# FFN entry by token halves, weight tiles between modulation chunks, and modulation sums a few tiles later, in a one-layer decoder kernel on one Trainium2 core

## The chip, the cores and the metric

The kernel runs on one core of one Trainium2 chip. The time is the device time of one execution in microseconds. Before the change it is 1890.21 us, the median of three runs (1888.95, 1891.62 and 1890.21). TensorE multiplies, ScalarE (ACT) and VectorE (DVE) work on tiles in SBUF and PSUM, GpSimd (POOL) does small work here, and SyncE (SP) issues all loads. PE stands for TensorE in the profile.

## The reference

One decoder layer over 256 tokens of width 2048, in float32:

```
mod = silu(c) @ w_ada + b_ada                     # 6 x 2048: shift, scale, gate for mixer and FFN
h = rmsnorm(x) * g * (1 + sc_m) + sh_m
y = token_mixer(h)                                # HGRN2 recurrence and latent attention from one projection,
                                                  # each with an output projection, sigmoid-gated sum, @ w_out
x = x + ga_m * rmsnorm(y)
h = rmsnorm(x) * g * (1 + sc_f) + sh_f
y = (silu(h @ w_gate) * (h @ w_up)) @ w_down      # inner width 5632
x = x + ga_f * rmsnorm(y)
```

## The kernel before

**Products.** Activations are kept transposed, channels on the partitions: `hT_hi` and `hT_lo` hold 16 blocks of 128 channels by 256 tokens. Each float32 product is made of three matmuls in a shorter format: high by high, high by low, low by high. So each weight tile (`raw`, 128 x 1024, two blocks of 128 channels by 512 columns, 512 KB) is loaded by SyncE, turned into `whi` by ScalarE (function `high`, line 465) and into `wlo` by VectorE (function `low`, line 1225), and multiplied by TensorE for both token halves (function `multiply`, lines 839 to 841): 2 halves x 2 blocks x 3 = 12 matmuls of 512 columns. A group of tiles (8 for 2048 channels) accumulates in a pair of PSUM banks, one bank for each half of 128 tokens; two pairs take turns.

**The ring.** There are four slots of `raw`, `whi` and `wlo` (`RING`). SyncE requests tile c when `low` of tile c - 4 is done (semaphore `lo_ready`); `high` of tile c waits for its landing and until tile c - 4 has been multiplied (`multiplied`). ScalarE and VectorE run three tiles ahead (`AHEAD`).

**Order.** Nothing is scheduled at run time: each engine's program is a written list of steps numbered by tile, with side work tied to a tile number. All engines work in order, so whatever stands behind a waiting instruction of its engine waits too. SyncE is one such queue.

**First phase** (up to about 250 us). Four quarters of 20 tiles. Each needs the shift and scale of its channels: 16 modulation chunks of 512 KB (`ada0`, function `load_ada0`) are multiplied by `silu(c)` and accumulated by VectorE (line 1232), and summed over the partitions by 16 matmuls of one column (`sum_rows`, line 874). There are ten chunk slots. SyncE requests 16 chunks, weight tiles 0 to 3, ten more chunks, the key weights and the masks (lines 367, 368), and then one tile at a time with as many chunks as `ada_due` lets VectorE consume. The sum of the second quarter follows tile 13.

**Output projections.** 32 tiles each, for attention (`place_om`, about 834 to 942) and recurrence (`place_oh`, up to 1035). Beside them, 16 chunk pieces each of later modulation columns are accumulated: VectorE takes piece r after `low` of tile `ADA_OM[r]` or `ADA_OH[r]`; SyncE requests it four tiles after piece r - 2 was taken. There are two chunk slots. TensorE sums after tile 23, VectorE reads the sums (`piece`) at step 26 or 27. At tile 8 of the second projection SyncE requests x once more (2 MB, into `att`, called `x2`).

**FFN entry.** The last projection (`place_out`, 32 tiles of `w_out`) ends at 1122.9 us. Then ScalarE squares the last outputs (line 704), VectorE applies a gain (1650), sums, and with POOL takes the reciprocal root (`rsqrt_of`, 1284 and 792), mixes in the residual (`x2`, 1682), ScalarE squares x2 (`square_sum`, 476), a second root gives two diagonal matrices (`by_rms`, 1688), and TensorE multiplies x2 with them (function `transpose_x2`, 1143): this transposes and normalises, 8 pairs of channel blocks with 8 instructions each. ScalarE applies scale and shift (735) and makes the high part (739), VectorE the low part (1694). The first gate tile is multiplied when the first pair is ready; pairs 4 to 7 are transposed after gate tiles 0 to 3.

Of the kernel before, what the change touches and what calls it, by code (L numbers as in the profile page):

```python
# [30 lines left out]
P = 128  # L31
# [26 lines left out]
ADA_SLOTS = 10  # L58
ADA_PACE = [(0, 0), (15, 16), (20, 21), (35, 32), (55, 48), (80, 48)]
# [55 lines left out]
def build(nc, x, vectors, consts, masks, positions, ada0, ada1, ada2, ga_bias, post_rows, w_start, w_kr, w_uqn, w_uqr, w_uk, w_uv, w_hf,  # L115
          w_hq, w_hi, w_hg, w_omla, w_ohg, w_out, w_gate, w_up, w_down, out):
    ctx = ExitStack()
    with ctx:
# [181 lines left out]
        ADA_OH = [4, 5, 6, 7, 8, 9, 10, 12, 13, 14, 15, 17, 18, 20, 21, 22]  # L300
# [32 lines left out]

        block = ctx.enter_context(nc.Block())
# [3 lines left out]
        def _(sp):  # L338
# [119 lines left out]
        def _(act):  # L458
# [249 lines left out]
            for c in range(GD * CD + AHEAD):  # L708
# [7 lines left out]
                if i == 3 and j == 1:  # L716
                    copy_gain(0)

            for tt in range(TT):
                act.wait_ge(sig("x_mixed"), tt + 1)  # L720
                if tt:
                    act.wait_ge(sig("x2_squared"), tt)
                square_sum(x2[:, tt], all_dec, stat[:, 10 + tt:11 + tt]).then_inc(sig("x2_squared"), 1)
            first = Place(B_FF, G_FF)
            for kp in range(KD // 2):
                if kp == 0 or kp > AHEAD:
                    high(first, max(kp, AHEAD))
                act.wait_ge(sig("scale_h_ready"), PH + 1)
                act.wait_ge(sig("x2_transposed"), kp + 1)
                if kp >= 2:  # L730

                    act.wait_ge(sig("h2_low"), kp - 1)
                for j in range(2):
                    k = 2 * kp + j
                    nc.scalar.activation(dec[:, kp % 2, j * T:(j + 1) * T], PS[:, XA + kp % 4, j * T:(j + 1) * T],
                                         ACT.Identity, scale=scale_h[:, k:k + 1], bias=mods[:, SH_F + k:SH_F + k + 1])\
                      .then_inc(sig("h2_scaled"), 1)
                act.wait_ge(sig("h2_scaled"), 2 * kp + 2)
                nc.scalar.activation(pairs(hT_hi, kp), dec[:, kp % 2, 0:NW], ACT.Copy)\
                  .then_inc(sig("h2_high"), 1)  # L740
# [47 lines left out]
        def _(pool):  # L788
# [22 lines left out]
            power(stat[:, 8:8 + TT], TT, "trunk", 1)  # L811

# [1101 lines left out]
```

## Time and profile before

| | |
|---|---|
| median of three runs | 1890.21 us |
| profiled execution, its own time | 1886.96 us |
| its span | 1885.1 us |
| TensorE busy | 1822.5 us (97%) |
| VectorE busy | 1296.2 us (69%) |
| ScalarE busy | 891.3 us (47%) |
| GpSimd busy | 104.3 us (6%) |
| loaded from HBM | 420.36 MB, 224 GB/s over the span |

The span runs from the first to the last instruction of one profiled execution; all positions in the text are microseconds from its start. A busy TensorE is not TensorE at full speed: its matmuls take twice as long where the granted clock is 0.50. What bounds the kernel is read from where TensorE waits, for whom, and where its clock is low.

### The profile page before, as it was taken

To read this page: it belongs to the slowest core of one execution; us is meant where nothing else is said; L and a number is where in the kernel's file an instruction comes from. 1 tells how busy PE (TensorE), PEld (TensorE's weight loads), DVE (VectorE), ACT (ScalarE), POOL (GpSimd) and SP (SyncE) were. 2 spreads that over 40 slices of the span, in tenths; PEclk is the share of its full clock that TensorE was granted. 3 is DMA by queue.
4 is the path that set the end of the run, shared out by engine and by line. 5 is a ranking of instruction groups with operands and counts; after the bars stand their busy time and mean duration, and the time that the engine had idled before them with its cause. 6 is when DMAs were issued, how large, how long until landed. Compare 5 with 4: busy or idle time off the path is not lost.

```text
span 1885.1 us, 24326 instructions
## 1 busy us (share of the span) xinstructions
PE 1822.5 (97%) x8828; PEld 1529.7 (81%) x8828; DVE 1296.2 (69%) x1361; ACT 891.3 (47%) x1007; POOL 104.3 (6%) x72
## 2 busy tenths in 40 slices
PE   3999999999999999999999989999999999999997
PEld 2788888888888888888778867888888888888886
DVE  7799768678668668669677554666656666665557
ACT  5544555645645645644334446444443444443443
POOL 0000000120120120220000000000000000000000
PEclk9999999999999999999999999999999999999999
DMA  9997548646646647547786654666666666665553
GB/s 383 409 366 254 191 156 291 237 162 227 233 156 231 226 156 244 180 167 268 242 317 226 219 179 138 223 222 230 212 227 230 212 222 219 228 212 176 193 190 131
DMA packets 115985, 423.38 MB, mean 225 GB/s; under 512 B 13008, under 2 KB 13392, under 8 KB 115408
## 3 DMA queue, kind: packets, MB, share of 16 engines
q1 hardware_dynamic: 115920, 422.51, 65.3%
q8 instruction: 42, 0.69, 0.2%
q14 instruction: 23, 0.19, 0.0%
HBM read 420.36 MB, written 2.10 MB: 224 GB/s over the span
## 4 chain that ended last, share of the span: by engine, by line
PE 89%; DVE 5%; DMA 4%; issue 1%; ACT 1%; SPq 0%; POOL 0%; DVEq 0%; ACTq 0%; POOLq 0%
PE PS L839 27%; PE PS L841 26%; PE PS L840 26%; DMA ada_raw<-in_ada 2%; PE PS L986 2%; DVE ada_acc L1232 2%; DMA raw<-in_w_start 2%; PE PS L848 1%; DVE wlo L1225 1%; PE PS L874 1%; PE PS L1032 1%; PE PS L1031 1%; PE PS L1143 0%; PE PS L857 0%; PE PS L866 0%
## 5 line engine op out<-in xcount | busy, mean ns | idle before, releaser
L1225 DVE TENSOR_TENSOR wlo<-raw,whi 128x1024 fp32r<-128x1024 f32 x600 | 732.5, 1223 | 415.7 <-ACT whi L465 414.2
L465 ACT ACTIVATE whi<-raw 128x1024 fp32r<-128x1024 f32 x600 | 630.1, 1053 | 743.2 <-PE PS L841 658.3
L839 PE MATMUL PS<-whi,hT_hi 128*128 128x512 f32 x1792 | 707.6, 395 | 8.6 <-DVE wlo L1225 5.4
L841 PE MATMUL PS<-whi,hT_lo 128*128 128x512 f32 x1792 | 699.1, 390 | 0.0
L840 PE MATMUL PS<-wlo,hT_hi 128*128 128x512 f32 x1792 | 698.7, 390 | 0.0
L839 PEld LDWEIGHTS PS<-whi,hT_hi 128*128 128x128 f32 x1792 | 337.3, 188 | 77.9 <-issue 6.0
L841 PEld LDWEIGHTS PS<-whi,hT_lo 128*128 128x128 f32 x1792 | 336.9, 188 | 71.1
L840 PEld LDWEIGHTS PS<-wlo,hT_hi 128*128 128x128 f32 x1792 | 337.4, 188 | 67.4 <-issue 0.2
L839 PE MATMUL PS<-whi,cT_hi 128*128 128x512 f32 (+1 forms) x592 | 231.5, 391 | 2.0 <-DVE side L1549 1.5
L840 PE MATMUL PS<-wlo,cT_hi 128*128 128x512 f32 (+1 forms) x592 | 227.9, 385 | 0.0
L841 PE MATMUL PS<-whi,cT_lo 128*128 128x512 f32 (+1 forms) x592 | 227.9, 385 | 0.0
L1232 DVE SCALAR_TENSOR_TENSOR ada_acc<-ada_raw,csilu,ada_acc 128x512 f32<-128x512 f32 (+1 forms) x185 | 141.3, 764 | 32.5 <-DMA ada_raw<-in_ada 28.8
L839 PEld LDWEIGHTS PS<-whi,cT_hi 128*128 128x128 f32 x592 | 111.7, 189 | 25.9 <-issue 3.5
L841 PEld LDWEIGHTS PS<-whi,cT_lo 128*128 128x128 f32 x592 | 111.7, 189 | 22.3
L840 PEld LDWEIGHTS PS<-wlo,cT_hi 128*128 128x128 f32 x592 | 111.7, 189 | 21.9 <-issue 0.7
L1397 DVE TENSOR_TENSOR gate<-gate,PS 128x1024 f32<-128x1024 f32 x64 | 78.1, 1220 | 14.5 <-PE PS L841 14.2
L792 POOL TENSOR_TENSOR stat<-stat,con 128x2 f32<-128x2 f32 (+2 forms) x11 | 13.8, 1258 | 1329.4 <-DVE stat L1284 1211.7
L199 POOL TENSOR_TENSOR dec<-bT 128x512 f32<-128x512 f32 x24 | 47.1, 1964 | 392.8 <-DVE bT L1490 333.4
L1530 DVE COPY_PREDICATED pT<-msk,PS 128x512 f32<-128x512 uint8 x28 | 25.1, 896 | 33.6 <-issue 27.2
L986 PEld LDWEIGHTS PS<-zT 128*128 128x128 f32 x384 | 46.2, 192 | 1.6
L986 PE MATMUL PS<-zT 128*128 128x64 f32 x384 | 45.4, 271 | 0.0
L1752 DVE SCALAR_TENSOR_TENSOR gate<-ada_raw,csilu,gate 128x1024 f32<-128x1024 f32 x32 | 40.9, 1279 | 0.0
(228 smaller groups left out, 1052.0 us busy)
## 6 DMA issues: line engine op xcount, KB each, us to landing
ada_raw<-in_ada SPq DMA_DIRECT2D x142, 512.0 KB, 4.8
raw<-in_w_gate SPq DMA_DIRECT2D x88, 512.0 KB, 4.1
raw<-in_w_up SPq DMA_DIRECT2D x88, 512.0 KB, 4.2
raw<-in_w_down SPq DMA_DIRECT2D x88, 512.0 KB, 4.1
raw<-in_w_start SPq DMA_DIRECT2D x80, 512.0 KB, 4.9
raw<-in_w_hf SPq DMA_DIRECT2D x32, 512.0 KB, 3.9
raw<-in_w_hq SPq DMA_DIRECT2D x32, 512.0 KB, 5.0
raw<-in_w_hi SPq DMA_DIRECT2D x32, 512.0 KB, 4.5
```

Source lines behind the costliest of these rows:

```text
L199: eng.tensor_tensor(d[:, :, 1, :], b[:, :, 1, :], end, ALU.subtract)
L465: nc.scalar.activation(whi[:, pl.slot(c), 0:w], raw[:, pl.slot(c), 0:w], ACT.Copy)\
L839: nc.tensor.matmul(o, hi[:, kt, tok], whi[:, s, cols], start=start, stop=False)
L840: nc.tensor.matmul(o, hi[:, kt, tok], wlo[:, s, cols], start=False, stop=False)
L841: last = nc.tensor.matmul(o, lo[:, kt, tok], whi[:, s, cols], start=False, stop=stop)
L848: last = nc.tensor.transpose(PS[:, bank + h // 2, ((h % 2) * TT + tt) * P:][:, 0:P], src[:, tt, h * P:(h + 1) * P], ident)
L986: last = nc.tensor.matmul(PS[:, XA + L % 4, i * 64:(i + 1) * 64], z[:, i], zt[:, i, :, 1, :], start=True, stop=True)
L1225: nc.vector.tensor_tensor(wlo[:, s, 0:w], raw[:, s, 0:w], whi[:, s, 0:w].bitcast(F32), ALU.subtract)\
L1232: last = nc.vector.scalar_tensor_tensor(out=acc, in0=slot, scalar=csilu[:, a:a + 1], in1=acc, op0=ALU.mult, op1=ALU.add)
L1397: nc.vector.tensor_tensor(dst, dst, banks(2 * p), ALU.add).then_inc(pair_free[p], 1)
L1530: nc.vector.copy_predicated(o, mask.unsqueeze(1).broadcast_to(shape), PS[:, XA + L % 4, :].rearrange("p (i x m) -> p i x m", i=2 * HPG, m=m))\
L1752: nc.vector.scalar_tensor_tensor(out=acc, in0=ada_raw[:, q % 2], scalar=csilu[:, bass.ds(n * 2 + (q // 2 - 2), 1)], in1=acc, op0=ALU.mult, ...
```

## The change

There are three parts.

First phase: SyncE requests three chunks (`ADA_FIRST`) behind weight tiles 0 to 3 and not ten; from then on, the lead of the chunk requests grows by one with every third tile, up to ten. Key weights and masks are requested after tile 24.

Output projections: in the first, the sum follows tile 25 and not 23, goes to PSUM bank `XA + 3`, and is read at step 27. In the second, the chunk pieces are taken at other tiles, the sum follows tile 26, and is read at step 28. The waits of the row transposes that use these banks move with them.

FFN entry: the last four tiles of `w_out` are multiplied for the first 128 tokens (`tt` = 0), all four, and then for the other 128. Squares, gain, root, mixing, squares of x2, root and diagonal are done for each half by itself. The first four channel pairs are transposed, scaled and split for each half by itself (list `H2`: 8 half units, then 4 whole ones), and gate tiles 0 to 3 are multiplied first for half 0, then for half 1. ScalarE's and VectorE's orders are written out anew.

```diff
+ADA_FIRST = 3
-        ADA_OH = [4, 5, 6, 7, 8, 9, 10, 12, 13, 14, 15, 17, 18, 20, 21, 22]
+        ADA_OH = [6, 7, 8, 9, 10, 13, 14, 15, 17, 18, 21, 22, 23, 24, 25, 26]
+        H2 = [(kp, slice(tt * P, (tt + 1) * P)) for tt in range(TT) for kp in range(4)] + [(kp, slice(0, T)) for kp in range(4, KP)]
...
-            for a in range(KD, KD + ADA_SLOTS):
+            asked = KD + ADA_FIRST
+            for a in range(KD, asked):
                 load_ada0(a)
-            sp.dma_start(key_weights, w_kr).then_inc(sig("kr_loaded"), 16)
-            sp.dma_start(msk[:], masks).then_inc(sig("masks_loaded"), 16)
...
-                    for a in range(KD + ada_due(c - RING) + ADA_SLOTS, KD + ada_due(c - RING + 1) + ADA_SLOTS):
-                        if a < ADA0:
-                            load_ada0(a)
+                    ahead = KD + ada_due(c - RING + 1) + min(ADA_SLOTS, ADA_FIRST + (c - RING) // 3)
+                    for a in range(asked, min(ahead, ADA0)):
+                        load_ada0(a)
+                    asked = max(asked, min(ahead, ADA0))
+                    if c == SG * W_G + RING:
+                        sp.dma_start(key_weights, w_kr).then_inc(sig("kr_loaded"), 16)
+                        sp.dma_start(msk[:], masks).then_inc(sig("masks_loaded"), 16)
```

ScalarE after tile 31 of `w_out` (`square_out_rows` squares one half of the last outputs, `square_x2` one half row of x2, `h2_high` scales and converts one unit):

```diff
+            square_out_rows(0)
+            high(first, 0)
+            high(first, 1)
+            square_x2(0, 0)
+            square_x2(0, 1)
+            square_out_rows(1)
+            high(first, 2)
+            h2_high(0)
+            h2_high(1)
+            square_x2(1, 0)
+            h2_high(2)
+            square_x2(1, 1)
+            h2_high(3)
+            high(first, 3)
+            for u in range(4, 8):
+                h2_high(u)
+            for u in range(8, len(H2)):
+                high(first, u - 4)
+                h2_high(u)
```

TensorE (`multiply_rows` is `multiply` for one half):

```diff
-                if c == 23:
+                if c == 25:
                     pe.wait_ge(ada_step, ADA0 + 2 * S_OM + 2 * ADA_N)
                     for r, acc in enumerate(ada_sum):
-                        last = sum_rows(acc, XA, r * HPG)
+                        last = sum_rows(acc, XA + 3, r * HPG)
...
-            for c in range(N_ST):
+            for c in range(N_ST - RING):
...
+            for tt in range(TT):
+                for kp in range(CD - RING, CD):
+                    hi, lo, home = row_home(2 * KP + kp)
+                    last = multiply_rows(pl, GD - 1, CD, (GD - 1) * CD, kp, tt, hi, lo, kt0=KC * (home - kp))
+                    if tt:
+                        last.then_inc(multiplied, 1)
+                if tt == 0:
+                    last.then_inc(sig("out_rows"), 1)
...
+            for u in range(4):
+                transpose_x2(u)
+            for c in range(4):
+                if c == 3:
+                    for u in range(4, 8):
+                        transpose_x2(u)
                 pe.wait_ge(sig("h2_low"), c + 1)
+                multiply_rows(first, 0, CD, 0, c, 0, hT_hi, hT_lo)
+            for c in range(4):
+                pe.wait_ge(sig("h2_low"), 4 + c + 1)
+                multiply_rows(first, 0, CD, 0, c, 1, hT_hi, hT_lo).then_inc(multiplied, 1)
+                transpose_x2(8 + c)
+            for c in range(4, CD):
+                pe.wait_ge(sig("h2_low"), 4 + c + 1)
                 multiply(first, 0, CD, 0, c, c + 1, hT_hi, hT_lo)
```

VectorE (`y_rms` and `x2_rms` are the roots of one half, the gain multiply of the half stands inside `y_rms`; `mix_x2` mixes half a row of one half):

```diff
+            y_rms(0)
...
+            mix_x2(0, 0)
+            mix_x2(0, 1)
+            low(first, 0)
+            x2_rms(0)
+            y_rms(1)
+            dve.wait_ge(pair_free[1], freed_by(1, G_FF))
+            mix_x2(1, 0)
+            low(first, 1)
+            h2_low(0)
+            mix_x2(1, 1)
+            h2_low(1)
+            low(first, 2)
+            h2_low(2)
+            x2_rms(1)
+            h2_low(3)
+            low(first, 3)
             dve.wait_ge(sig("scale_h_ready"), PH + 1)
+            for u in range(4, 8):
+                h2_low(u)
+            for u in range(8, len(H2)):
+                low(first, u - 4)
+                h2_low(u)
```

## Rows read from the trace of the kernel before

**Rows 1.** The page, part 1: busy us, share of span, count of instructions.
```profile
PE 1822.5 (97%) x8828; PEld 1529.7 (81%) x8828; DVE 1296.2 (69%) x1361; ACT 891.3 (47%) x1007; POOL 104.3 (6%) x72
```

**Rows 2.** Busy time by stretch: stretch, its length, busy us by engine, clock, DMA.
```profile
105.00:850.00 745.00, 743.51 (x3949) 635.74 (x3948) 554.93 (x649) 399.64 (x485) 93.06 (x61) 1.00 0.63 214
...
1157.00:1870.00 713.00, 713.00 (x3184) 590.15 (x3184) 441.69 (x369) 294.27 (x286) 3.53 (x1) 1.00 0.63 210
```

**Rows 3.** Waits of TensorE: total us, times, longest us.
```profile
PE PS L839 <- DVE wlo L1225: 5.9, 4, 3.0
PE PS L874 <- DVE ada_acc L1232: 4.2, 2, 2.8
```

**Rows 4.** Timeline of TensorE where it waits: start, us, instruction, [wait before <- releaser].
```profile
54.70 0.47 PE L839 MATMUL PS<-whi,hT_hi 128*128 128x512 f32 x1 [3.00 <-DVE wlo L1225]
...
82.80 1.95 PE L874 MATMUL PS<-con,mixed 128*128 128x1 f32 x16 [0.64 <-DVE mixed L1232]
...
907.72 1.95 PE L874 MATMUL PS<-con,ada_acc 128*128 128x1 f32 x16 [1.46 <-DVE ada_acc L1232]
...
958.67 0.47 PE L839 MATMUL PS<-whi,hT_hi 128*128 128x512 f32 x1 [1.78 <-DVE wlo L1225]
...
968.05 0.50 PE L839 MATMUL PS<-whi,hT_hi 128*128 128x512 f32 x1 [0.65 <-DVE wlo L1225]
```

**Rows 5.** Busy time by stretch around low clocks (third last column: PEclk).
```profile
54.70:58.10 3.40, 3.40 (x15) 2.83 (x16) 3.25 (x3) 1.81 (x2) 0.00 (x0) 1.00 1.03 411
82.80:86.20 3.40, 3.40 (x23) 3.15 (x24) 3.40 (x4) 2.52 (x3) 0.00 (x0) 1.00 1.03 411
909.70:913.10 3.40, 3.40 (x9) 2.63 (x9) 2.57 (x4) 0.00 (x0) 0.00 (x0) 0.50 0.92 287
...
1134.90:1138.40 3.50, 3.45 (x16) 3.48 (x17) 1.23 (x2) 1.28 (x3) 0.00 (x0) 0.50 0.31 112
1138.40:1141.80 3.40, 3.40 (x25) 3.14 (x25) 1.38 (x2) 3.34 (x7) 0.00 (x0) 1.00 0.10 39
```

**Rows 6.** Timelines of ScalarE and VectorE, first phase.
```profile
52.24 1.06 ACT L465 ACTIVATE whi<-raw 128x1024 fp32r<-128x1024 f32 x1 [10.91 <-DMA raw<-in_w_start]
...
80.07 2.67 DVE L1232 SCALAR_TENSOR_TENSOR mixed<-ada_raw,csilu,mixed 128x1024 f32<-128x1024 f32 x2
```

**Rows 7.** Second projection: request and landing of x; timeline of VectorE.
```profile
att<-in_x SPq DMA_DIRECT2D x1, 2048.0 KB, 10.4
...
907.58 2.35 DVE L1225 TENSOR_TENSOR wlo<-raw,whi 128x1024 fp32r<-128x1024 f32 x2
...
955.84 1.54 DVE L1232 SCALAR_TENSOR_TENSOR ada_acc<-ada_raw,csilu,ada_acc 128x512 f32<-128x512 f32 x2 [5.81 <-DMA ada_raw<-in_ada]
957.30 1.22 DVE L1225 TENSOR_TENSOR wlo<-raw,whi 128x1024 fp32r<-128x1024 f32 x1
```

**Rows 8.** Timelines of ScalarE, VectorE and TensorE at the FFN entry.
```profile
1120.28 1.06 ACT L465 ACTIVATE whi<-raw 128x1024 fp32r<-128x1024 f32 x1 [1.66 <-PE PS L841]
1122.94 0.60 ACT L704 ACTIVATE dec<-PS 128x512 f32<-128x512 f32 x1 [1.60 <-PE PS L841]
...
1126.79 4.62 DVE L1682 SCALAR_TENSOR_TENSOR att<-gate,stat,att 128x2048 f32<-128x2048 f32 x2 [0.81 <-POOL stat L792]
...
1131.43 1.91 ACT L476 ACTIVATE dec<-att 128x2048 f32<-128x2048 f32 x1 [0.26 <-DVE att L1682]
...
1134.95 5.45 PE L1143 MATMUL PS<-stage,att 128*128 128x128 f32 x32 [12.04 <-DVE stage L1688]
...
1137.09 1.02 ACT L735 ACTIVATE dec<-PS,mods,scale_h 128x256 f32<-128x256 f32 x2 [2.71 <-PE PS L1143]
...
1138.71 1.02 ACT L735 ACTIVATE dec<-PS,mods,scale_h 128x256 f32<-128x256 f32 x2
...
1151.05 0.48 PE L839 MATMUL PS<-whi,hT_hi 128*128 128x512 f32 x1
...
1154.68 0.47 PE L839 MATMUL PS<-whi,hT_hi 128*128 128x512 f32 x1
```

More of the change, by code:

```diff
@@ L706, in square_out @@
                       .then_inc(sig("y_squared"), 1)
-            for c in range(GD * CD + AHEAD):
+            for c in range(GD * CD):
                 high(pl, c)
@@ L717, in _, with square_out_rows @@
                     copy_gain(0)
-            for tt in range(TT):
-                act.wait_ge(sig("x_mixed"), tt + 1)
+            first = Place(B_FF, G_FF)
+            junk = side[:].rearrange("p t c -> p (t c)")
+            def square_out_rows(tt):
                 if tt:
[L722 to L727, printed above, removed]
+                    act.wait_ge(multiplied, pl.through(N_ST - 1))
+                    act.wait_ge(sig("x2_squared"), 2)
+                else:
+                    act.wait_ge(sig("out_rows"), 1)
+                act.wait_ge(sig("y_squared"), (GD - 1) * TT + tt)
+                nc.scalar.activation(junk[:, 0:NW], PS[:, 2 * pl.pair(GD - 1) + tt, :], ACT.Square,
+                                     accum_out=sums[:, tt, GD - 1:GD]).then_inc(sig("y_squared"), 1)
@@ L1124, in _, with multiply_rows @@
             pl = place_out
-            for c in range(N_ST):
+            def multiply_rows(pl, g, n, c0, c, tt, hi, lo, kt0=0):
+                p = pl.pair(g)
+                if c == 0 and tt == 0:
+                    pe.wait_ge(pair_free[p], pl.freed(g))
+                pe.wait_ge(lo_ready, pl.through(c0 + c))
+                s = pl.slot(c0 + c)
+                for k in range(KC):
+                    kt = kt0 + c * KC + k
+                    tok = slice(tt * P, (tt + 1) * P)
+                    cols = slice(k * NW, (k + 1) * NW)
+                    o = PS[:, 2 * p + tt, :]
+                    start, stop = c == 0 and k == 0, c == n - 1 and k == KC - 1
+                    nc.tensor.matmul(o, hi[:, kt, tok], whi[:, s, cols], start=start, stop=False)
+                    nc.tensor.matmul(o, hi[:, kt, tok], wlo[:, s, cols], start=False, stop=False)
+                    last = nc.tensor.matmul(o, lo[:, kt, tok], whi[:, s, cols], start=False, stop=stop)
+                return last
+            for c in range(N_ST - RING):
                 if c == CD:
@@ L1653, in gain_pair @@
                   .then_inc(pair_free[p], 1)
-            for c in range(AHEAD, GD * CD + AHEAD):
+            for c in range(AHEAD, GD * CD):
                 low(pl, c)
@@ L1680, in _, with gain_rows_out @@
-            dve.wait_ge(pair_free[1], freed_by(1, G_FF))
-            for tt in range(TT):
-                nc.vector.scalar_tensor_tensor(out=x2[:, tt], in0=ya[:, tt], scalar=stat[:, 8 + tt:9 + tt],
-                                               in1=x2[:, tt], op0=ALU.mult, op1=ALU.add)\
-                  .then_inc(sig("x_mixed"), 1)
-            dve.wait_ge(sig("x2_squared"), TT)
-            rsqrt_of(stat[:, 10:10 + TT], D, "trunk", 2)
-            for tt in range(TT):
+            def gain_rows_out(tt):
+                if tt:
+                    dve.wait_ge(multiplied, pl.through(N_ST - 1))
+                else:
+                    dve.wait_ge(sig("out_rows"), 1)
+                cols = slice((GD - 1) * NW, GD * NW)
+                p = pl.pair(GD - 1)
+                nc.vector.tensor_tensor(ya[:, tt, cols], PS[:, 2 * p + tt, :], post_gain[0][:, cols], ALU.mult)\
+                  .then_inc(pair_free[p] if tt else sig("y_scaled"), 1)
@@ L1689, in _ @@
                   .then_inc(sig("rms_diagonal"), 1)
[L1690 to L1701 removed]
+            first = Place(B_FF, G_FF)
```

108 lines of the change are left out of this document (62 added, 46 removed).

## The prediction

> **What bounds the kernel now.** Read the engine shares first: TensorE is busy for 1822.5 of 1885.1 us [rows 1], so whatever the change gives has to come out of the remaining 62.6 us or out of stretches at half clock. The busy time by stage then shows where not to look: from 105 to 850 us TensorE misses 1.5 us of 745, from 1157 to 1870 nothing of 713 [rows 2]. The table of waits then names, beside the start: 5.9 us in four waits for a low weight half, 4.2 us in two waits for modulation sums [rows 3]. The timeline of TensorE places those that the diff can reach: 3.00 us at 54.70, 0.64 at 82.80, 1.46 at 907.72, 1.78 at 958.67 and 0.65 at 968.05 [rows 4]; the fourth wait for a low half is what is left of the 5.9, 0.5 us, and 12.04 us stand at 1134.95, before the transposes of the FFN entry [rows 8]. (The 2.8 us that are left of the 4.2 lie before the first weight tile is multiplied and are not edited.) Last, the granted clock by stretch: 1.00 after the wait of 3.00 us, but 0.50 from 909.7 to 913.1 and in the first 3.5 us after work restarted at 1134.9, then 1.00 [rows 5].
>
> So a tile's 12 matmuls set the pace: on ScalarE 1.06 us of work and 1.66 us of waiting for TensorE make 2.72 us a tile [rows 8]. ScalarE's conversion and VectorE's subtraction (1.22 us, [rows 7]) hide in that, and only the places above pay.
>
> **First phase.** Before, ten modulation chunks, the key weights and the masks stand in SyncE's queue between weight tile 3 and tile 4. At 411 GB/s [rows 5] a 512 KB piece takes 1.28 us, so that is 11.1 pieces or 14.3 us; ScalarE waits 10.91 us for tile 4's landing at 52.2 [rows 6], and TensorE 3.00 us. After, three chunks stand there: tile 4 lands 8.1 pieces or 10.4 us earlier, near 42, and is no longer late. The sum behind the 0.64 us waits for VectorE's last two chunks of the second quarter, 80.07 to 82.74 [rows 6]; these follow the subtraction of tile 14. Ahead of that tile stand 15 weight and 20 chunk pieces plus 1.1 of key weights and masks now, 15 and 16 after: 5.1 pieces, 6.5 us sooner, less what the DMA engines idle because tiles 5 to 7 wait for free ring slots (three handovers of about 1 us: I take 2.5). Net 4 us sooner against the 3.0 us by which TensorE comes sooner, so this wait goes too: 3.64 us. No matmul, conversion or byte is removed. What is late next is tile 26: there the lead of the chunks is back at ten, the key weights have been requested, and the DMA backlog is as before while TensorE is 3.6 us ahead. Before, tile 26 was needed near 117.2 (84.6 after the sum, 12 tiles of 2.72); its piece is the 44th behind tile 4's, landing near 52.2 + 56.3 = 108.5 before and after; with 2.5 us of idle 111.0, with conversion and subtraction 113.4, against a need at 113.6. Nothing to spare, so the bound is 1.6 us lost again. I take 3.6, ends 2.0 and 3.7.
>
> **Modulation sums of the output projections.** The first sum moves from tile 23 to tile 25 and to another bank. Its last chunk ends on VectorE just before 907.72 [rows 4]; TensorE would now reach the sum at 906.3 + 2 x 2.72 + 0.6 of transposes = 912.3, so the 1.46 us go. The subtractions of tiles 25 and 26 end at 908.7 and 909.9 [rows 7], each before its turn (909.0, then after the sum). The half clock behind the sum goes with the wait, I think: the stretch of 3.4 us at half clock [rows 5] does 1.7 us of work. After the wait of 0.64 us with the same 16 one-column matmuls at 82.80 the clock stayed at 1.00 [rows 5], and the new sum has no wait at all. Gain 3.2, ends 1.4 (clock still falls) and 3.2. The added wait is VectorE's read of the sum at step 27, for which it now stands some 3 us; behind it are a gating multiply and the subtraction of tile 28, which end about 2.7 us after TensorE starts tile 26, two tiles before tile 28 is due. SyncE's next request waits for that subtraction and lands within its 11 us of ring.
>
> In the second projection the chunks move two tiles later at the start, so that chunk pieces 2 and 3 are requested with tiles 10 and 11 and not 8 and 9, behind the 2 MB of x, which take 10.4 us to land [rows 7]. Before, VectorE stood 5.81 us for such a piece at 955.84 [rows 7], with tile 8's subtraction queued behind it. After, tile 8's subtraction comes at about 951, before any chunk that x delays; x ends near 949.5, tiles 9 and 10 at 950.7 and 952.0, the next piece at 953.3, each further one at 1.28 us, or 4 after its request. Worked on, subtractions 9 to 12 end at 956.0, 958.7, 962.7 (a gated pair of 1.2 us each follows) and 966.2; TensorE needs them at 959.4, 962.1, 964.9 and 967.6. Slack 3.4, 3.4, 2.2, 1.4: all three waits, 1.78 + 0.65 + 0.5 = 2.9 us, go. Six chunks in a row (21 to 26) let VectorE fall behind by some 0.5 us a tile, 3 of its 5.7 us of lead, and the sum now waits until after tile 26. I take 2.9, ends 1.0 and 2.9.
>
> **FFN entry.** Call the end of the last output tile T (1122.9). Before: squares, gain, reciprocal root, mixing (4.62 us for two rows of 2048), squares of x2 (1.91 each), a second root and two diagonals follow one another, 12.04 us to the first transpose; 32 transpose instructions take 5.45 us mostly at half clock, and the fifth gate tile starts at 1154.68 [rows 8], T + 31.8.
>
> After, the last four output tiles run token half 0 first, so its outputs are whole at T - 5.44. By the durations of [rows 8]: square 0.60 and the reading of its sum, 0.75 (T - 4.65); reduce, scale and root 1.3 (T - 3.3), the half's gain multiply (0.65 by the 1.22 for 1024) beneath it; two mixings of 1024 at 1.28 [rows 6] (T - 0.8); ScalarE's squares of them 1.25 each, the last at T + 0.75; reduce, scale, POOL, diagonal 1.6: T + 2.35. The first transposes start there: 9.7 us less waiting. Then VectorE's queue sets the pace: y's root for half 1, its gain multiply, a mixing (T + 4.7), subtraction of gate tile 1 (T + 5.85), and only then the first low part of h2: tile 0, half 0, at T + 6.3. A mixing and a low part put tile 1 at T + 7.9, a subtraction and a low part tile 2 at T + 9.45. ScalarE (1.62 us from one whole unit to the next; a half has 512 elements less in its three instructions, at 0.85 ns by the squares of 512 and 2048: 1.18 us) ends half 1's squares at T + 9.0; root and diagonal T + 10.9; 16 transposes 1.8 (T + 12.75); tile 3's half 1.36, T + 14.1. From there TensorE has all its operands: four halves 5.44 and four transpose units at 3.63 - 2.72 = 0.9, 3.6 in all, so the fifth gate tile starts at T + 23.1. That is 8.7 us sooner at full clock. Work is the same: 64 transposes, 96 matmuls; about 5.5 us of waits remain.
>
> What the clock adds: waits of about 2.35 and 2.1 us stand around 1.8 us of transposes. Rows speak both ways: full clock after 3.00 us of waiting, half after 1.46 us and a sum [rows 4, 5]. One stretch of 3.4 us at half clock costs 1.7 us less the small waits that it fills. I take 1.2, nearest to one stretch; the lower end is two stretches, 3.4. If half-size instructions cost ScalarE as much as whole ones, four units lose 1.8 us more. Entry: 7.5, ends 8.7 - 3.4 - 1.8 = 3.5 and 8.7.
>
> **Sum.** 3.6 + 3.2 + 2.9 + 7.5 = 17.2 us. The profiled execution took 1886.96 us for its span of 1885.1, so it would be 1869.8. The median of the runs is 1890.21, 3.25 above: 1873.0.
>
> **The rivals.**
> A, chance 15%: the entry gains only about 3.5. For it: VectorE carries both halves' chains and the weight subtractions in one queue, and TensorE works in pieces of 1.4 us at an uncertain clock. Against: half 0's chain ends before T. 1873.0 + 4.0 = 1877.0.
> B, 13%: waits move rather than go in the early parts: tile 26 is late by 1.6, the sum is followed by the low clock (1.7), the second projection keeps 1.9. 1873.0 + 5.2 = 1878.2.
> C, 4%: every short piece of the entry runs at half clock: two times four half units of transposes, 1.8 each, and three halves of tiles, 4.1, once more, of which 0.8 fills waits, 6.9 lost, so the entry gains 1.8: 1873.0 + 5.7 = 1878.7. For it: the half clock behind a wait and a sum at 909.7; against it: 1.00 behind 3.00 us of waiting [rows 5]. The Trainium skill (TensorE: Matmul & The Clock Gate, section HAM oscillation) describes this: matmul groups shorter than the waits between them start at the low clock each time. The row at 909.7 agrees, that at 54.7 does not.
> D, 2%: the change does not do what it says: the low part of half 0 comes after half 1's mixing, and the entry is no shorter. With B's losses, 1873.0 + 7.5 + 5.2 = 1885.7.
> E, 3%, slower: stop and go keeps the clock at half from the first transposes to the end of the gate group. That is 1.8 + 1.8 + 5.4 + 5.4 + 3.6 + 10.9 = 28.9 us of work, once more 28.9, less 4 us that fill waits, against the 1.2 in my sum: 1873.0 + 23.7 = 1896.7. It decides from some 18 us more than forecast, so about 22 us of such work at half. Against it: the clock was back 3.5 us after the restart at 1134.9 [rows 5].
> The forecast keeps 63%, with its own range of 1869.5 to 1876.5.
>
> **From these to the numbers.** Cases are told apart from no change at about 0.2%, 3.8 us. Forecast, A, B and C are faster, 0.95, of which I give 0.01 to what none of them names; within 0.2%, or just at its line, is D and that: 0.03; slower is E: 0.03. The range reaches up past A, B and C, and down by 3.5: the terms at their good ends give 1.3, and single runs of one kernel differ by up to 2.7 (1888.95 to 1891.62). So 1869.5 to 1880.5.
>
> **What will show it.** No wait above 0.3 us on TensorE between 50 and 100 us; none before the sum near 912, and a clock of 1.00 behind it; none between 950 and 970. At the entry, first transposes 2.3 us after the last output matmul, three or four waits summing to 5.5 us, at most one stretch at 0.50, and the fifth gate tile 23 to 25 us after T. Wrong would be: a wait near tile 26 of the first phase, VectorE still in the mixing of half 1 when T + 6.3 has passed, or a clock of 0.50 beyond T + 12.

## The result, and the profile after

The changed kernel takes 1869.12 us, median of four runs (1867.67 to 1872.3), against 1889.58 us for the kernel before (four runs, 1888.45 to 1891.62): ratio 0.9893, 95% interval 0.9876 to 0.991. It is faster, by 20.5 us. The forecast was 1873.0 with a range of 1869.5 to 1880.5, so the time lies 0.4 us below the range: the direction was right and the gain was put too low. Its own single runs spread over 4.6 us, more than that distance.

The profiled execution after took 1872.3 us, the slowest of its four, and that of before, 1886.96, lay under all its other first runs. The two profiles are therefore only 14.7 us apart. The experiments below give each kernel a second profile, and the reading rests on both pairs.

The page after, part 1:
```profile
PE 1823.1 (97%) x8828; PEld 1531.2 (82%) x8828; DVE 1296.6 (69%) x1373; ACT 893.8 (48%) x1023; POOL 105.0 (6%) x74
```
TensorE has the same 8828 matmuls as in [rows 1] and works as long; the span is shorter because it waits less. Its waits between 30 and 1200 us, after (total us, times, longest):
```profile
PE PS L891 <- issue: 3.0, 1, 3.0
PE PS L926 <- DVE ada_acc L1319: 2.2, 1, 2.2
PE PS L1222 <- DVE stage L1786: 2.2, 1, 2.2
PE PS L891 <- DVE side L1636: 1.5, 3, 0.5
PE PS L891 <- DVE stage L1484: 1.2, 1, 1.2
PE PS L1191 <- DVE hT_lo L1794: 1.0, 1, 1.0
PE PS L891 <- DVE side L1484: 0.8, 1, 0.8
PE PS L891 <- DVE wlo L1312: 0.3, 1, 0.3
```
Of [rows 3], the 5.9 us for low weight halves are down to 0.3, and of the 4.2 us for modulation sums the 2.2 at the start are left. The wait of 12.04 us at the entry [rows 8] has become 2.2 and 1.0. Two rows are new, both for L1484: VectorE's addition of a finished pair of banks to `stage` or `side`, which frees the pair.

The timeline of TensorE after, at the places of [rows 4, 8]:
```profile
40.37 0.77 PE L891 MATMUL PS<-whi,hT_hi 128*128 128x512 f32 x1 [3.01 <-issue]
...
80.26 1.84 PE L926 MATMUL PS<-con,mixed 128*128 128x1 f32 x16
...
110.63 0.50 PE L891 MATMUL PS<-whi,hT_hi 128*128 128x512 f32 x1 [1.16 <-DVE stage L1484]
...
117.21 0.50 PE L891 MATMUL PS<-whi,hT_hi 128*128 128x512 f32 x1 [0.81 <-DVE side L1484]
...
139.13 1.06 PE L926 MATMUL PS<-con,ada_acc 128*128 128x1 f32 x9
...
909.53 0.50 PE L891 MATMUL PS<-whi,cT_hi 128*128 128x512 f32 x1 [0.29 <-DVE wlo L1312]
...
917.36 0.60 PE L909 MATMUL PS<-con,mixed 128*128 128x128 f32 x4
...
990.46 0.71 PE L909 MATMUL PS<-con,gate 128*128 128x128 f32 x5
...
1117.94 2.64 PE L1222 MATMUL PS<-stage,att 128*128 128x128 f32 x16 [2.21 <-DVE stage L1786]
1121.56 0.80 PE L1191 MATMUL PS<-whi,hT_hi 128*128 128x512 f32 x1 [0.98 <-DVE hT_lo L1794]
...
1140.02 0.48 PE L891 MATMUL PS<-whi,hT_hi 128*128 128x512 f32 x1
```
No wait stands at tile 4, at the sum of 80.26, or in the second projection. The first transposes of the FFN entry start 2.21 us behind the last output product, the fifth gate tile (1140.02) 24.3 us behind it, where it was 31.8.

Busy time by stretch after (stretch, length, busy us by engine, clock, DMA share, GB/s); it answers to [rows 5]:
```profile
909.70:913.10 3.40, 3.40 (x20) 2.85 (x20) 2.04 (x2) 0.95 (x2) 0.00 (x0) 1.00 0.66 186
1119.17:1126.00 6.83, 5.85 (x19) 4.63 (x18) 6.14 (x11) 6.70 (x17) 0.54 (x1) 0.50 0.31 109
1126.00:1129.40 3.40, 3.40 (x23) 3.05 (x22) 1.26 (x2) 1.25 (x4) 0.00 (x0) 1.00 0.37 136
```
At 909.7 TensorE does 20 matmuls in 3.4 us at full clock where it did 9 at half; at the entry 6.83 us are at half clock.

### The profile page after: what moved, and what is told of

Read it like the earlier page. It is cut to its first block and busy times, and to the rows that moved or that the text cites. A ratio compares the mean times of both kernels' runs of the same rounds, so it can differ in the third digit from the quotient of the medians.

```text
span 1870.4 us, 24368 instructions
## 1 busy us (share of the span) xinstructions
PE 1823.1 (97%) x8828; PEld 1531.2 (82%) x8828; DVE 1296.6 (69%) x1373; ACT 893.8 (48%) x1023; POOL 105.0 (6%) x74
## 5 line engine op out<-in xcount | busy, mean ns | idle before, releaser
L891 PE MATMUL PS<-whi,hT_hi 128*128 128x512 f32 x1760 | 694.3, 395 | 5.0 <-issue 3.0
L893 PE MATMUL PS<-whi,hT_lo 128*128 128x512 f32 x1760 | 686.2, 390 | 0.0
L892 PE MATMUL PS<-wlo,hT_hi 128*128 128x512 f32 x1760 | 685.8, 390 | 0.0
L891 PEld LDWEIGHTS PS<-whi,hT_hi 128*128 128x128 f32 x1760 | 331.0, 188 | 72.6 <-issue 3.3
L893 PEld LDWEIGHTS PS<-whi,hT_lo 128*128 128x128 f32 x1760 | 330.8, 188 | 69.8
L892 PEld LDWEIGHTS PS<-wlo,hT_hi 128*128 128x128 f32 x1760 | 331.2, 188 | 66.4 <-issue 0.2
L845 POOL TENSOR_TENSOR stat<-stat,con 128x1 f32<-128x1 f32 (+2 forms) x13 | 14.6, 1123 | 1318.3 <-DVE stat L1371 1200.5
L1484 DVE TENSOR_TENSOR gate<-gate,PS 128x1024 f32<-128x1024 f32 x64 | 78.0, 1218 | 14.6 <-PE PS L893 14.3
```

The costliest lines, as they stand in the source:

```text
L891: nc.tensor.matmul(o, hi[:, kt, tok], whi[:, s, cols], start=start, stop=False)
L892: nc.tensor.matmul(o, hi[:, kt, tok], wlo[:, s, cols], start=False, stop=False)
L893: last = nc.tensor.matmul(o, lo[:, kt, tok], whi[:, s, cols], start=False, stop=stop)
L1484: nc.vector.tensor_tensor(dst, dst, banks(2 * p), ALU.add).then_inc(pair_free[p], 1)
```

## The experiments

The kernel before had a median of 1888.86 us in the first group of runs (15 runs), 1887.97 in the second (9) and 1888.85 in the third (27). Each ratio is against it.

**The changed kernel once more.** No edit.

> The changed kernel once more. Theory (the sum by parts is right on the traces, and single executions differ by where the clock's half-speed stretches fall at the start of the span): median again about 20 us under before, single times spread over 3 to 5 us, and the profiled one need not lie at the median. In its trace the waits of the FFN entry and of tiles 24 to 26 of the first phase return within 0.2 us, while the first weight tile starts anywhere from 38.5 to 40.5 us. Rival (one of the two profiled executions was not typical in a part after the start): the fifth gate tile or the output projections come at another distance, by over 1 us, from what stands before them.

1869.1 us (1868.13 to 1870.61), ratio 0.99 (0.9885 to 0.9915). The times and the waits at tiles 24 and 26 (1.1 and 0.9 us) came back as the theory said. At the entry the rival is right: the second wait is 0.4 us and not 1.0, and the fifth gate tile starts 22.6 us behind the last output product, where it was 24.3.

**The kernel before once more.** No edit.

> The kernel before, once more, for a second profile. Theory 1 (its first profile was a cheap execution): the times lie at 1888.9 like the other runs of before; this profile shows the same waits of the matrix engine as the first (2.66 at 54.70, 2.1 at 82.80, 1.48 at 907.7, some 2.9 in four behind the second projection) and other stretches at half clock, 20 to 31 us of them ahead of the last where the first had 20.5. Rival (the profile costs time or saves it in every execution): its waits are the same too, but so are the half stretches, and the time again lies 2 to 3 us under the median of the unprofiled runs.

1889.53 us (1885.77 to 1891.14, ten runs), ratio 1.0003 (0.9994 to 1.0012); its profiled execution took 1887.94. The times lie where the other runs of before do, and the clock differs, so theory 1 holds for the clock. It does not for the waits: the one before tile 4 is 0.83 us where the first profile had 3.00, since this execution starts its first weight tile at 40.40 and that one at 38.60. TensorE in this second profile of before, timeline and then stretches:
```profile
40.40 0.76 PE L839 MATMUL PS<-whi,hT_hi 128*128 128x512 f32 x1 [3.01 <-issue]
54.11 0.47 PE L839 MATMUL PS<-whi,hT_hi 128*128 128x512 f32 x1 [0.83 <-DVE wlo L1225]
...
909.37 2.10 PE L874 MATMUL PS<-con,ada_acc 128*128 128x1 f32 x16 [1.53 <-DVE ada_acc L1232]
...
958.18 0.39 PE L841 MATMUL PS<-whi,cT_lo 128*128 128x512 f32 x1
960.11 0.47 PE L839 MATMUL PS<-whi,hT_hi 128*128 128x512 f32 x1 [1.54 <-DVE wlo L1225]
960.42 0.40 PE L840 MATMUL PS<-wlo,hT_hi 128*128 128x512 f32 x1
960.66 0.39 PE L841 MATMUL PS<-whi,hT_lo 128*128 128x512 f32 x1
960.89 0.40 PE L839 MATMUL PS<-whi,hT_hi 128*128 128x512 f32 x1
...
1135.77 5.69 PE L1143 MATMUL PS<-stage,att 128*128 128x128 f32 x32 [12.04 <-DVE stage L1688]
```
```profile
85.00:88.41 3.41, 3.41 (x10) 2.67 (x9) 3.38 (x6) 2.25 (x4) 0.00 (x0) 0.50 1.02 406
...
911.02:914.43 3.41, 3.41 (x10) 2.76 (x10) 2.92 (x4) 0.00 (x0) 0.00 (x0) 0.50 0.75 222
...
1126.06:1139.71 13.65, 3.94 (x18) 3.97 (x19) 7.19 (x10) 6.69 (x9) 1.39 (x2) 0.50 0.14 47
```
Behind the sum at 82.8 the clock falls here, from 85.00 to 88.41 (ten matmuls in 3.41 us); in the profile the forecast was made from it stayed at 1.00 over 82.8 to 86.2 with 23 [rows 5]. Six profiles have the old first phase (two of before, and those of the kernels below that leave it alone). All reach this sum at 82.7 to 82.8, however early they start. In four the clock falls at 84.6 to 85.2, and the third sum follows 57.9 us behind this one; in the other two it follows 56.3 us behind. So this stretch costs 1.6 us when it comes, and the forecast was made from an execution without it. Before the last stretch this execution has 30.7 us at half clock (10.24 at the start, 3.41, 3.41, 13.65), the first profile of before had 20.5 (6.83, 3.41, 10.24), the two of after 17.1 and 10.2. The mean granted clock lay between 0.989 and 0.993 in all runs of before, between 0.994 and 0.997 in all of after.

The gain by stage, each the difference of the starts of the same instruction in two traces (third modulation sum, 139.13 above; transposes four tiles behind the first projection, 917.36; transposes in the third projection, 990.46; fifth gate tile, 1140.02):

| stage | forecast | first profiles | second profiles |
|---|---|---|---|
| first phase | 3.6 | 0.0 | 2.0 |
| first projection sum | 3.2 | 2.6 | 3.2 |
| second projection | 2.9 | 4.6 | 3.8 |
| FFN entry | 7.5 | 7.5 | 9.5 |
| all | 17.2 | 14.7 | 18.5 |

The two pairs differ by 2.0 us in the first phase because of the 1.6 us at half clock behind the sum and 0.3 us by which the two executions of the changed kernel differ. Other profiles show how far one pair can be trusted. The third sum comes at 139.1 to 140.8 us with the old first phase (six profiles) and at 138.2 to 140.8 with three early chunks (five). The stretch with the second projection is 3.8 to 5.2 us shorter in each profile with the new list. The fifth gate tile follows 31.8 to 32.6 us behind the last output product with the old entry (six) and 22.6 to 24.3 with the new one (four profiles without further edits there).

**The three parts alone**, each put into the kernel before.

```diff
-            for a in range(KD, KD + ADA_SLOTS):
+            asked = KD + ADA_FIRST
+            for a in range(KD, asked):
```

> The kernel before with the first part alone: three chunks behind tiles 0 to 3, key weights and masks after tile 24. Theory of the first trace (waits near tiles 24 and 26 take back what tile 4's wait gave): 1.9 us faster, with waits of about 1.2 and 0.8 us there. Rival (the forecast, 3.6 us): no wait between 50 and 135 us, and 3.6 us faster.

1887.79 us (1883.01 to 1888.05, eleven runs), ratio 0.9992 (0.9983 to 1.0001): 1.1 us, not told apart from nothing; 3.6 us lie outside the interval, 1.9 inside. In its trace the wait at tile 4 is gone, and waits of 1.15 us at 109.45 and 1.02 us at 116.25 stand in its place, as in the whole change.

```diff
-        ADA_OH = [4, 5, 6, 7, 8, 9, 10, 12, 13, 14, 15, 17, 18, 20, 21, 22]
+        ADA_OH = [6, 7, 8, 9, 10, 13, 14, 15, 17, 18, 21, 22, 23, 24, 25, 26]
...
-                if c == 23:
+                if c == 25:   # first sum; the second one: c == 26
```

> The kernel before with the second part alone: sums after tiles 25 and 26, chunk pieces of the second projection at the later tiles. Theory of the first trace (each wait costs some 0.3 us beyond what it shows, since the pipeline empties and fills): 2.6 us from the first projection, 4.6 from the second, 7.2 in all. Rival (the forecast by the waits alone): 6.1 us. Third: the second projection's gain came from the rest of the change and not from its own tile numbers: under 4 us.

1879.97 us (1879.24 to 1880.84), ratio 0.9957 (0.9943 to 0.9971): 8.9 us where 6.1 were forecast for the two terms; the interval is 5.5 to 10.8 us, so the times alone do not rule out 6.1. In its trace the transposes in the third projection come 7.2 us sooner than in the second profile of before. No wait is left between 850 and 1000 us.

```diff
-            for kp in range(4):
-                transpose_x2(kp)
-            for c in range(CD):
+            for u in range(4):
+                transpose_x2(u)
+            for c in range(4):    # token half 0, then half 1, then whole tiles
```

> The kernel before with the third part alone: FFN entry by token halves. Theory: 7.5 us faster, the fifth gate tile 24.3 us after the last output matmul, two stretches at half clock. Rival (unprofiled executions keep the clock up at the entry, which would explain a median gain above the sum by traces): 9 to 11 us faster.

1880.28 us (1879.6 to 1880.44), ratio 0.9958 (0.9944 to 0.9971): 8.6 us; 7.5 were forecast, and the interval of 5.5 to 10.6 us holds both theories. The trace was expected to show two half stretches and the fifth gate tile at 24.3 us; it shows one (3.41 us) and 23.05. The three alone add up to 18.5, all together give 19.8 (1888.86 less 1869.1): within the intervals the parts are independent.

**The sums one at a time.** The first sum alone (`c == 23` to `25`, other bank, its reading at 27):

> The kernel before with the later modulation sum of the first output projection alone (sum behind tile 25 into another bank, piece at 27). Theory 1 (each wait that goes is worth what the trace shows plus 0.3 us, and the half clock that it brings): the wait of 1.48 and the half stretch at 909.7 go, a gain of 3.3 us at the first sum of the second projection, none behind it: 1885.6. Rival (this sum has no part of its own, half clock comes there anyway): 1.5 us, 1887.4.

1884.98 us (1883.25 to 1887.29, eleven runs), ratio 0.9976 (0.9967 to 0.9985): 3.9 us. Then the second list and sum alone:

> The kernel before with the spread list and the later sum of the second output projection alone (sum behind tile 26, piece at 28). Theory 1 (the four waits go, 2.9 us as shown and 0.3 us each on top, and nothing is late in their place): 4.3 to 4.6 us, 1884.5, and with the other sum alone 7.9 to 8.9 together. Rival (the gain of 4.6 behind tile 12 in the kernel with both comes in part from the first sum, which frees VectorE earlier): 2.9 us, 1886.0, and one wait of over 0.5 us stays in the second projection.

1884.66 us (1882.88 to 1886.93, eleven runs), ratio 0.998 (0.9971 to 0.9989): 4.2 us. Waits of TensorE from 850 to 1000 us, first of the one, then of the other kernel:
```profile
PE PS L839 <- DVE wlo L1225: 4.2, 4, 1.7
```
```profile
PE PS L874 <- DVE ada_acc L1232: 1.2, 1, 1.2
```
With the first sum alone the sum's own wait is gone, and the waits of the second projection are longer than the 2.8 us they were: TensorE comes sooner to the same late chunks. With the second list alone none of them is left. For the second list theory 1 holds (4.3 to 4.6 expected): its trace is 4.2 us ahead of the second profile of before at the third projection, and no wait is left, which speaks against the rival of 2.9, though the interval (2.1 to 5.5 us) does not. For the first sum the time speaks for theory 1 (3.3 expected, 1.5 outside the interval of 2.8 to 6.2), but the claim that nothing follows is wrong by 1.4 us of waits: its trace, of an execution 2.3 us above its median, gains 2.5 us up to the transposes behind the first projection and is only 1.1 ahead at the third. How the median comes to 3.9 is open.

**More chunks early.** The new waits of the first phase should come of idle DMA engines between 42 and 57 us.

```diff
-ADA_FIRST = 3
+ADA_FIRST = 6
```

> The changed kernel with six chunks and not three behind weight tiles 0 to 3 (ADA_FIRST = 6). Theory: the waits near tiles 24 and 26 stem from 4.5 us in which the DMA engines had nothing asked of them between 42 and 57 us, since each request waited for a ring slot; three more chunks (3.8 us) fill that, tile 4 lands near 45 and is still not late, and both waits go: 2.3 us faster than the changed kernel, some 1867. Rival: VectorE's queue makes them (a chunk and the addition of a group stand ahead of each subtraction): they stay, 1869. Rival: a wait before tile 4 returns, and nothing is gained.

1867.75 us (1866.99 to 1870.94), ratio 0.9897 (0.9882 to 0.9913), at most 1.4 us under the changed kernel by medians and within its interval. The DMA engines from 40 to 60 us in slices of half a microsecond (GB/s, and the total), first after, then with six chunks:
```profile
GB/s 393 377 123 33 8 131 295 377 393 418 377 98 131 188 336 369 451 410 410 377 377 303 287 377 377 361 344 377 418 385 426 393 426 418 410 434 426 410 418 401
DMA packets 1844, 6.73 MB, mean 337 GB/s; under 512 B 204, under 2 KB 204, under 8 KB 1843
```
```profile
GB/s 410 426 410 401 402 418 401 418 401 426 410 401 401 410 410 418 401 426 410 410 377 410 401 434 401 410 393 426 401 401 418 418 402 418 393 426 401 402 418 426
DMA packets 2243, 8.19 MB, mean 410 GB/s; under 512 B 246, under 2 KB 246, under 8 KB 2242
```
Three chunks leave two holes, near 41 to 43 and 45.5 to 47 us: 337 of 410 GB/s over 20 us, that is 3.6 us of transfers not made. Six fill them. Then one wait is left between 45 and 135 us, and the third sum starts 3.0 and 2.7 us sooner than in the two profiles of the change. The theory of idle DMA engines holds for the waits; of the 2.3 us that it promised, the medians show 1.4 at most, and the ratios, each against its own group of runs, 0.5:
```profile
79.80 1.95 PE L926 MATMUL PS<-con,mixed 128*128 128x1 f32 x16 [0.60 <-DVE mixed L1319]
...
136.12 1.06 PE L926 MATMUL PS<-con,ada_acc 128*128 128x1 f32 x9
```

**A busy TensorE in the entry's first wait.**

```diff
+            pe.wait_ge(lo_ready, first.through(0))
+            for i in range(9):
+                nc.tensor.matmul(PS[:, XA + 3, :], hT_hi[:, i % 4, 0:P], whi[:, first.slot(0), 0:NW], ...)
```

> The changed kernel with nine matmuls of 512 columns, whose result nobody reads, in TensorE's first wait at the FFN entry (2.0 us of the 2.2). Theory: the half clock at the entry comes of TensorE's doing nothing; with work there it stays at 1.00, and the fifth gate tile comes 22.0 to 22.6 us after the last output matmul in each execution, against 24.3 and 22.6 in the two traces so far: 1 us faster in the median. Rival: the later wait and the short pieces are enough to drop it: no change. Rival: the first transposes come later by the added work and the time rises by up to 0.5 us.

1869.65 us (1868.31 to 1872.25), ratio 0.9901 (0.9886 to 0.9916). TensorE at the entry, timeline and stretches:
```profile
1117.55 2.32 PE L1229 MATMUL PS<-whi,hT_hi 128*128 128x512 f32 x9 [0.23 <-DVE wlo L1315]
1119.70 1.95 PE L1222 MATMUL PS<-stage,att 128*128 128x128 f32 x16
1123.16 0.50 PE L1191 MATMUL PS<-whi,hT_hi 128*128 128x512 f32 x1 [1.51 <-DVE hT_lo L1797]
...
1139.96 0.48 PE L891 MATMUL PS<-whi,hT_hi 128*128 128x512 f32 x1
```
```profile
1116.00:1119.50 3.50, 3.27 (x15) 2.39 (x14) 2.07 (x7) 3.31 (x7) 0.55 (x1) 1.00 0.27 64
1119.50:1123.00 3.50, 2.15 (x18) 1.91 (x16) 3.40 (x5) 2.81 (x8) 0.54 (x1) 1.00 0.22 88
```
The clock stays at 1.00 here, and the fifth gate tile starts 22.6 us behind the last output product (1139.96 less 1117.3). The second profile of the change, with one stretch of 3.41 us at half clock, has 22.6 too; two more profiles with one stretch have 23.1 (six chunks, and the entry alone); the first, with 6.83 us, has 24.3. So one stretch costs 0 to 0.5 us, since full clock mostly turns into waiting for VectorE, and two cost 1.7. The gain of 1 us that was expected of the median did not come. Both edits together:

> The kernel after with six early modulation chunks in place of three and nine idle matrix products of 512 columns in the first wait at the FFN entry. Theory 1 (both edits keep what they gave: 1.3 us in the first phase; at the entry the fifth gate tile 22.6 us behind the last product of the output, against 22.6 with one half stretch and 24.3 with two): 1867.3, 0.5 under first6. Rival (the idle products only take power or issue time: no gain on an average execution): 1868.3. If the gain of first6 was chance of the executions: 1869.1.

1868.15 us (1867.32 to 1868.95), ratio 0.9893 (0.9878 to 0.9908): nothing over six chunks alone, though the granted clock was 1.00 without a break from 44.38 to 1860.27. The rival holds.

**A busy TensorE at the start.** 10 and 14 idle transposes in the two waits before the first weight tile.

```diff
+            keep_busy(10)
             sum_quarter(0)
             pe.wait_ge(sig("xT_copied"), KD // 2)
+            keep_busy(14)
```

> The changed kernel with 24 transposes whose result nobody reads before the first modulation sum (10) and before the first weight tile (14), where TensorE waits 2.2 to 3.1 and 3.0 us. Theory: the clock then stays up from there on; the first 12 to 16 matmuls, now at half, and the sum take 3 us less between them: 2 to 3 us faster, and the single times lie within 2 us of each other, as the alignment of a half-speed stretch no longer matters. Rival: the transposes run at half clock themselves and push the sum and the first tile back: no change, or 1 us slower.

1876.47 us (1874.18 to 1877.26), ratio 0.9937 (0.9923 to 0.995): 7 us slower than the change. The stretch from 36.11 to 42.93 is at 0.50 all the same, though the 14 transposes run from 35.38 on. Up to the third sum (137.83) this profile is still 1.0 and 1.3 us ahead of the two of the change. Then two waits are new, in the loop over the groups:
```profile
495.18 0.79 PE L891 MATMUL PS<-whi,hT_hi 128*128 128x512 f32 x1 [2.11 <-issue]
...
639.28 0.49 PE L891 MATMUL PS<-whi,hT_hi 128*128 128x512 f32 x1 [1.84 <-issue]
```
Stretches of 6.8 and 3.4 us at half clock stand there, and the two places cost 4.6 and 3.6 us against either profile of the change. The waits name no releaser ("issue"), but the trace shows one. In both, TensorE is at the branch that closes the loop (`pe.Fori`, line 1118): it takes 4.02 us at 490.90 and 3.75 us at 635.26, where the same branch takes 0.24 and 0.22 in the changed kernel. And the DMA queue that loads instructions, from 480 to 770 us, reads
```profile
q8 instruction: 18, 0.29, 0.4%
```
while none of the other 13 profiles has a single row of it there: they load seven blocks of 16 KB between 330 and 480 us, in the first turn of the loop, and none in the next two. So the loop's code, which had stayed in place, is loaded again in every turn. The loop itself was not edited; that the instructions ahead of it shifted its code across a block is the likely reason, and was not tried.

**One subtraction earlier.** The subtraction of gate tile 1 goes between the scaling and the root of half 0.

```diff
-            x2_rms(0)
+            x2_rms(0, lambda: low(first, 1))
...
-            low(first, 1)
```

> The changed kernel with the subtraction of gate tile 1 moved, on VectorE, from behind the first mixing of half 1 into its wait for POOL's root of half 0. Theory (VectorE's queue sets the pace of the entry): the first transposes come 0.5 us later, everything from the first low part on 0.6 us earlier, and the second wait of TensorE shrinks by 1 us: 0.6 us faster. Rival (the clock or ScalarE sets the pace from there on): no change. Third: TensorE's first wait grows by 0.5 us and brings a further stretch at half clock: 1 us slower.

1870.29 us (1869.13 to 1872.8), ratio 0.9905 (0.989 to 0.992): no gain. The first transposes wait 3.13 us and not 2.2, the second wait is gone, and the fifth gate tile comes 23.4 us behind the last output product (1140.60 less 1117.15), between the two profiles of the change. The first low part of h2 starts 5.2 us behind that product instead of 5.4, so the 0.6 us that VectorE was to save there is 0.2.

## Why the prediction came out as it did

**The last step failed: 3.25 us added to a sum made from one execution.** The gains were read from an execution of before of 1886.96 us and then set against a median of 1890.21; the 3.25 us between the two were added back as if the change left them alone. The runs show two things in them. First, 1.35 us: the median of three runs stood that far above the 1888.86 of 15 later ones. Second, the remaining 1.9 us: the profiled execution had less half clock than most. Its mean granted clock was 0.993. Of 61 later runs of before only two have that (median 1887.33), 28 have 0.990 (median 1889.75) and 3 have 0.989 (1891.76). The places are known from the profiles: the stretch behind the sum at 82.8, 1.6 us, in four of six profiles and not in that one; and the entry, where that profile is 0.2 to 0.8 us quicker than the other five. Both stand behind waits that the change removes, so what they cost is gain and not offset. That they make up the whole 1.9 us is not shown.

In numbers, the miss of 3.9 us (1873.0 to 1869.1) is the 1.35 us and 2.55 us of gain not forecast (19.75 less 17.2). Without the added term the forecast would have been 1869.8, 0.7 us off; that is partly luck, since the terms were wrong too, in both directions: against the parts alone, the first phase was put 2.5 us too high, the projections 2.8 and the entry 1.1 too low, and 1.2 us come when all are together.

**First phase, 3.6 us: mis-sized, 1.1 alone.** The wait at tile 4 went. The one at the sum went in the first profile of the change and is 0.86 us at 79.89 in the second; the sum comes 2.5 and 2.9 us sooner. But from there to the third sum the changed kernel takes 58.9 us where 56.3 do without half clock: the waits at tiles 24 and 26 (1.16 and 0.81 us as printed) take back 2.6 us, all of that gain in the first pair. The sum had 1.6 us for this loss only as its lower end (2.0). What stays is the half clock behind the sum, 1.6 us in an execution of before that has it, none in one that has not; that is why the first pair shows 0.0 and the second 2.0. The term failed in the DMA engines' idle time, for which I took 2.5 us: it is 3.6, and with six chunks, which fill it, both waits are gone. Tile 26 had nothing to spare. It was late, and tile 24 with it, by another road than the lower bound took: ScalarE's conversion of tile 24 waits for its landing, VectorE for the conversion, then does a chunk, and the addition that frees the pair of banks comes behind both. ScalarE, then VectorE after, timelines:
```profile
105.93 1.06 ACT L484 ACTIVATE whi<-raw 128x1024 fp32r<-128x1024 f32 x1 [1.51 <-DMA raw<-in_w_start]
```
```profile
107.02 1.23 DVE L1312 TENSOR_TENSOR wlo<-raw,whi 128x1024 fp32r<-128x1024 f32 x1 [1.34 <-ACT whi L484]
108.16 1.28 DVE L1319 SCALAR_TENSOR_TENSOR ada_acc<-kT,csilu,ada_acc 128x1024 f32<-128x1024 f32 x1
109.36 1.22 DVE L1484 TENSOR_TENSOR stage<-stage,PS 128x1024 f32<-128x1024 f32 x1
```
A start that comes late is absorbed by such waits. The first weight tile of before began at 38.60 in one profile and at 40.40 in the other; tile 4 came at 54.70 and 54.11, and the sum at 82.80 and 82.81. After, nothing absorbs it at tile 4: a start of 40.37 against 39.24 reaches the sum, where VectorE's chunk (0.86 us of waiting in the second profile) leaves 0.4 of it.

**First projection sum, 3.2: right within what single executions differ** (2.6, 3.2, and 3.9 alone). The wait went (0.29 us for a low half stand at 909.53 in the first profile), the clock stayed at 1.00 behind the sum, and VectorE stands 2.96 us for its reading, 3 forecast, without harm:
```profile
914.70 0.17 DVE L1336 TENSOR_TENSOR mods<-PS,vec 128x8 f32<-128x8 f32 x1 [2.96 <-PE PS L926]
```

**Second projection, 2.9: too small** (4.6, 3.8, and 4.2 alone). All waits went, as forecast. I paid for each only what the trace prints beside it. In the second profile of before, products in a row start 0.23 us apart (960.66, 960.89). Around a printed wait of 1.54 the starts are 1.93 apart (958.18, 960.11), since the wait is counted from the printed end of the product before it, and the next one follows after 0.31 (960.42). So a wait that goes gives 1.70 + 0.08 = 1.78 us, 0.24 more than is printed. The three waits of that profile print 2.8 us and are worth 3.6 so counted, of 3.8 measured. The first profile has two more late starts that the table of waits does not print (964.38 and 983.81, 0.3 us each), which makes its gain the larger one.

**FFN entry, 7.5: its size at full clock was right, the 1.2 us taken off for the clock were too much** (7.5, 9.5, and 8.6 alone). First transposes 2.35 us behind the last output product forecast, 2.21 and 2.22 measured; first low part of h2 ready at 6.3, measured 5.8 (1121.51 less 1115.73). The waits sum to 3.2 us (2.6 in the second profile), not 5.5. The fifth gate tile was put at 23.1 by the full-clock sum. It came at 22.6 with the clock kept up, at 22.6 to 23.1 in three profiles with one half stretch, and only in the first profile of the change, with two (6.83 us), at 24.3. So that the first pair gives just 7.5 is luck: its execution of before was the quickest of six at the entry, and that of after the slowest. The rule cited under rival C (the Trainium skill, TensorE: Matmul & The Clock Gate, section HAM oscillation) is borne out in its direction: with shorter waits there was less half clock at the entry (3.4 to 6.8 us against 10.2 to 13.7), and the idle products removed it. The restored clock was worth nothing here, because VectorE's queue decides when TensorE goes on.

**The rivals.** A (entry 3.5): no, 7.5 to 9.5. B (waits move): true in the first phase alone, and larger than its 1.6 us there: 2.6. C and E (half clock through the entry): 3.4 to 6.8 us at 0.50, no more. D: the change does what it says. The range failed at its lower end. The two figures given for it, 1.3 us for the terms and 2.7 for single runs, add up to 4.0, and 3.5 was taken; 4.0 would have reached 1869.0. Neither figure was for the half clock that a typical execution of before loses.

**Best version.** Six early chunks give 1867.75 us, the lowest median here, but its interval holds the changed kernel's ratio: a gain of 0.5 us by the ratios and 1.4 by the medians, which these runs do not settle.

## What to carry to other kernels

Before adding gains that were read from one profile to a median of runs, ask what the runs above it have more of: if it is half clock or waits at the places that the change touches, that difference goes with the change and is gain, not offset. Two profiles are not enough to size a term of 2 us: every kernel that leaves a stage alone is one more profile of that stage. Price a removed wait by the starts of the instructions on either side of it, not by the figure beside it. Where requests are taken out of a queue, check that what is left keeps the DMA engines at full rate. And when an edit slows down code that it does not touch, look at the branch that closes the loop and at the queue that loads instructions.

## What the runs showed of the hardware

Two executions of one kernel differ in where the clock falls: none or 3.41 us behind the sum at 82.8, with waits of 0.64 and 0.85 us before it, and 10.24 or 13.65 us around a wait of 12.04 us at the entry in both. TensorE kept at work through a wait of 2.2 us held 1.00 at the entry, in two kernels; 24 transposes in the waits at the start did not stop the fall at 36.11. And 24 transposes added between 30 and 38 us cost 7 us, at 495 and 639 us, in a loop that was not edited: its instructions were loaded again in each turn (18 blocks of 16 KB between 480 and 770 us, none in any other profile), and the branch that closes it took 4.02 and 3.75 us instead of 0.24 and 0.22.
